# The begin of a two-block transformer kernel: x in SP's queue, 128-column sums, turned rows by k-tile

## What is computed

```python
c_act = jax.nn.silu(c)
mod = c_act @ w_ada[l] + b_ada[l]
sh_m, sc_m, gt_m, sh_f, sc_f, gt_f = jnp.split(mod, 6, axis=-1)
h = modulate(rms_norm(x, g_mix[l]), sh_m, sc_m)
proj = jnp.einsum('bsd,de->bse', h, w_in[l])
qa, ka, va, qb, kb, vb, gate_logits = jnp.split(proj, splits, axis=-1)
```

## Time and profile before

| what | us |
|---|---|
| median of three runs | 1457.21 (1453.15 to 1458.4) |
| the profiled execution | 1455.16 |
| its span in the profile | 1453.3 |
| TensorE busy | 1398.8 |
| VectorE busy | 906.8 |
| ScalarE busy | 737.4 |

### The profile page before, as it was taken

One profiled execution on the slowest core, in us unless ns is written; L12 is line 12 of the kernel. 1 busy time (PEld: TensorE's weight loads), 2 busy tenths in 40 slices (PEclk: granted clock), 3 DMA queues, 4 the chain that ended last, 5 costly groups with the idle time before them and its releaser, 6 DMA issues.

```text
span 1453.3 us, 18520 instructions
## 1 busy us (share of the span) xinstructions
PE 1398.8 (96%) x7039; PEld 1160.8 (80%) x7039; DVE 906.8 (62%) x1171; ACT 737.4 (51%) x1013; POOL 84.8 (6%) x133
## 2 busy tenths in 40 slices
PE   5999998999999999999889999999999999999998
PEld 4877876899987888887768888888888877788886
DVE  5577786688876645468876645456454555764543
ACT  4457745644546443366466444455444466564342
POOL 3011100000000000022300000000000100000000
PEclk9999999999999999999999999999999999999999
DMA  9787654577653765534335756538565463566550
GB/s 354 273 312 236 207 170 149 171 242 247 234 175 124 238 191 186 178 131 145 116 106 178 253 177 200 181 106 279 176 200 177 136 217 116 174 218 195 181 174 29
DMA packets 177592, 274.31 MB, mean 189 GB/s; under 512 B 6466, under 2 KB 120898, under 8 KB 177506
## 3 DMA queue, kind: packets, MB, share of 16 engines
q1 hardware_dynamic: 170800, 250.87, 52.3%
q0 software_dynamic: 5552, 20.20, 4.5%
q10 hardware_dynamic: 1153, 2.07, 0.4%
HBM read 272.05 MB, written 1.06 MB: 188 GB/s over the span
## 4 chain that ended last, share of the span: by engine, by line
PE 49%; DVE 1%; ACT 1%; issue 0%; POOL 0%; DVEq 0%; POOLq 0%; ACTq 0%
PE psum L2466 15%; PE psum L2468 15%; PE psum L2467 15%; PE psum L2711 1%; PE psum L2635 1%; PE psum L2563 0%; PE psum L2664 0%; PE psum L2617 0%; DVE attn L2238 0%; PE psum L2616 0%; PE psum L2578 0%; POOL scr L1801 0%; ACT w_hi L1866 0%; DVE attn L2291 0%; ACT junk L1932 0%
## 5 line engine op out<-in xcount | busy, mean ns | idle before, releaser
L2065 DVE TENSOR_TENSOR w_lo<-raw,w_hi 128x2048 fp32r<-128x2048 f32 (+1 forms) x158 | 359.7, 2279 | 187.0 <-ACT w_hi L1866 186.3
L2466 PE MATMUL psum<-w_hi,hT_hi 128*128 128x512 f32 x912 | 366.7, 402 | 9.4 <-DVE hT_lo L2161 3.5
L1866 ACT ACTIVATE w_hi<-raw 128x2048 fp32r<-128x2048 f32 (+1 forms) x158 | 299.7, 1899 | 121.8 <-PE psum L2468 80.7
L2468 PE MATMUL psum<-w_hi,hT_lo 128*128 128x512 f32 x912 | 357.2, 392 | 0.0
L2467 PE MATMUL psum<-w_lo,hT_hi 128*128 128x512 f32 x912 | 357.1, 392 | 0.0
L2466 PEld LDWEIGHTS psum<-w_hi,hT_hi 128*128 128x128 f32 x912 | 172.8, 190 | 49.7 <-issue 12.6
L2468 PEld LDWEIGHTS psum<-w_hi,hT_lo 128*128 128x128 f32 x912 | 172.7, 189 | 37.1
L2467 PEld LDWEIGHTS psum<-w_lo,hT_hi 128*128 128x128 f32 x912 | 173.2, 190 | 33.7 <-issue 0.5
L2065 DVE TENSOR_TENSOR lo_qk<-raw,hi_qk 128x2048 fp32r<-128x2048 f32 (+1 forms) x35 | 79.3, 2264 | 40.2 <-ACT hi_qk L1866 40.1
L2065 DVE TENSOR_TENSOR lo_at<-raw,hi_at 128x2048 fp32r<-128x2048 f32 x35 | 80.2, 2290 | 35.4 <-ACT hi_at L1866 35.4
L2466 PE MATMUL psum<-w_hi,hc_hi 128*128 128x512 f32 x256 | 100.5, 393 | 0.8 <-DVE hc_lo L2386 0.4
(11 more groups left out here) (234 smaller groups left out, 2312.1 us busy)
## 6 DMA issues: line engine op xcount, KB each, us to landing
raw<-in_ffn_wg_dram SPq DMA_DIRECT2D x88, 512.0 KB, 3.9
raw<-in_ffn_wu_dram SPq DMA_DIRECT2D x88, 512.0 KB, 4.9
raw<-in_ffn_wd_dram SPq DMA_DIRECT2D x44, 1024.0 KB, 4.9
raw<-in_w_up_dram SPq DMA_DIRECT2D x44, 512.0 KB, 4.9
raw<-in_w_in_dram SPq DMA_DIRECT2D x19, 1024.0 KB, 7.2
ada_raw<-in_w_ada_dram POOLq DMA_DIRECT2D x24, 512.0 KB, 5.2
raw<-in_even_w_in_dram SPq DMA_DIRECT2D x12, 1024.0 KB, 5.0
raw<-in_odd_w_in_dram SPq DMA_DIRECT2D x12, 1024.0 KB, 5.1
```

The lines of the kernel that those rows point to most:

```text
L1866: nc.scalar.activation(hi_of(s), raw_of(s), ACT.Copy)\
L2065: nc.vector.tensor_tensor(lo_of(s), raw_of(s), hi_of(s).bitcast(F32), ALU.subtract).then_inc(lo_ready, 1)
L2466: nc.tensor.matmul(o, a_hi, b_hi, start=start, stop=False)
L2468: return nc.tensor.matmul(o, a_lo, b_hi, start=False, stop=stop)
```

## The change

- **Loads.** x is loaded by SP, between the first and the second part of `w_ada`, and no longer by POOL. The fourth early part comes in two loads of 512 KB with a semaphore for each half, and DVE waits for the second half ahead of its third operation.
- **Units.** `ka`'s first half and `qa`'s second half are each cut into two units of two k-tiles. Unit numbers shift: 0 and 1 are `qa`'s first half, 2 and 3 `ka`'s, 4 `va`'s, 5 and 6 `qa`'s second half, 7 `ka`'s, 8 `va`'s.
- **Column sums.** Both kinds of products have 128 equal columns instead of one, into 128 columns of the bank, and add up in place, so that DVE adds the bias in one operation instead of two.
- **Turned rows.** A group of two k-tiles gets a step for each k-tile: two pieces on ACT, one low part of 256 columns on DVE, and a count of its own for TensorE to wait on.
- **Warm products.** 24 in three places: eight after the condition vector, ten after the vectors are turned, six after the sums of round one.
- **Order.** The vectors are copied out by ACT; the statistics stand after the first part's sum. In round one the finish of sum 0 stands ahead of the last part of `w_ada`, and unit 1 is split between the two groups of turned rows. In round two all of `va`'s first half stands between the sums and turns.

```diff
+    pl.add("warm", bank=7, times=8)
+    st = tile_stat()
+    squared = x_squares(st, (0, 1), [("x_loaded", 16)] * TT)
+    pl.add("vectors", uses=vector_uses)
+    var(st, (0, 1), squared, False, EPS)
     shared = shared_ada(0, 0, 3)
-    vector_uses = [pl.use(b) for b in (4, 5, 6, 7)]
-    pl.add("vectors", uses=vector_uses)
-    st = x_stats([("x_loaded", 16)] * TT)
-    pl.add("warm", use=vector_uses[3], times=8)
+    pl.add("normalise", st=st, half=0)
+    pl.add("warm", bank=1, times=10)
+    turned_rows = [turn_early(G, ("scr_ready", scr_version()), ("mod", 1), ("mod", 0), 0, 2),
+                   turn_early(G, None, ("mod", 1), ("mod", 0), 2, 3)]
     ada(2, 0)
-    pl.add("normalise", st=st, half=0)
-    rest = turn_early(G, ("scr_ready", scr_version()), ("mod", 1), ("mod", 0), 0, (2, 3))
+    adasum(0, shared=shared)
     shared2 = shared_ada(2, 1, 3)
-    first = first_units([(0, 0, 2), (0, 2, 2), (1, 0, 4), (2, 0, 4), (0, 4, 4), (1, 4, 4), (2, 4, 4)])
+    first = first_units([(0, 0, 2), (0, 2, 2), (1, 0, 2), (1, 2, 2), (2, 0, 4), (0, 4, 2), (0, 6, 2), (1, 4, 4), (2, 4, 4)])
     pl.split_to(0)
-    adasum(0, shared=shared)
+    adasum(2, shared=shared2)
+    pl.add("warm", bank=0, times=6)
+    pl.add("modfinal", vec=1, gain=0, half=0)
+    turned_rows[0]()
     pl.split_to(1)
-    adasum(2, shared=shared2)
-    pl.add("modfinal", vec=1, gain=0, half=0)
-    rest[0]()
-    pl.split_to(2)
-    rest[1]()
+    turned_rows[1]()
+    pl.split_to(3)
...
-            pool.dma_start(X[:, :, :], x[0].rearrange("(t p) d -> p t d", p=P)).then_inc(x_loaded, 16)
...
+                    if e == 1:
+                        sp.dma_start(X[:, :, :], x[0].rearrange("(t p) d -> p t d", p=P)).then_inc(x_loaded, 16)
+                    if e % FIRST == FIRST - 1:
+                        sp.dma_start(view[:, 0:2, :], parts[0][2][:, 0:2, :]).then_inc(early_landed[e % FIRST], 16)
+                        sp.dma_start(view[:, 2:4, :], parts[0][2][:, 2:4, :]).then_inc(early_second, 16)
...
-                                nc.tensor.matmul(psum[:, use.bank, 4 + j:5 + j],
+                                nc.tensor.matmul(psum[:, use.bank, j * P:(j + 1) * P],
                                                  w[:, k * BANK + j * P:k * BANK + (j + 1) * P],
-                                                 c_act[:, 4 + k:5 + k], start=k == a["own"][0], stop=k == 3)
+                                                 c_act[:, 4 + k:5 + k].to_broadcast([P, P]),
+                                                 start=j == 0 and k == a["own"][0], stop=False, skip_group_check=True)
```

More of the change, by code:

```diff
@@ L351, in turn_group @@
         made = pl.turned_use(bank, buffered=bias is not None)
-        pl.add("turn", src=src, after=after, scale=scale, bias=bias, kt=kt, nk=nk, ts=ts, early=False, kept=None,
+        pl.add("turn", src=src, after=after, scale=scale, bias=bias, kt=kt, nk=nk, ts=ts, early=False, i0=0, kept=None,
                free=[hT_until[t] for t in ts if hT_until[t] is not None], **made)
@@ L356, in turn_group, with turn_early, go @@
                 G[k, t] = made["g"]
-    def turn_early(G, after, scale, bias, kt, banks):
-        later = []
-        for j, bank in enumerate(banks):
-            made = pl.turned_use(bank, buffered=True)
-            kw = dict(src="scr", after=after if j == 0 else None, scale=scale, bias=bias, kt=kt + 2 * j, nk=2, ts=(0, 1),
-                      kept=None, free=[], **made)
-            pl.add("turnrows", **kw)
-            later.append(kw)
-            for k in range(kt + 2 * j, kt + 2 * j + 2):
-                for t in range(TT):
-                    G[k, t] = made["g"]
-        return [lambda kw=kw: pl.add("turn", early=True, **kw) for kw in later]
+    def turn_early(G, after, scale, bias, kt, bank):
+        made = pl.turned_use(bank, buffered=True)
+        kw = dict(src="scr", after=after, scale=scale, bias=bias, ts=(0, 1), free=[], kept=None, **made)
+        pl.add("turnrows", kt=kt, nk=2, **kw)
+        pl.turned += 1
+        second = dict(kw, ti=pl.turned - 1, g=pl.turn(), buf_free=None)
+        made["use"].read_by = ("turned_ready", pl.turned)
+        pl.buffered[-1] = second["g"]
+        for t in range(TT):
+            G[kt, t], G[kt + 1, t] = made["g"], second["g"]
+        def go():
+            pl.add("turn", early=True, kt=kt, nk=1, i0=0, **kw)
+            pl.add("turn", early=True, kt=kt + 1, nk=1, i0=1, **second)
+        return go
     def turn(src, after, scale, bias, k0=0, nk=KT, banks=(4, 5, 6, 7), G=None):
@@ L1548, in program @@
         ada_landed = [sem(f"ada_landed{i}") for i in range(2)]
-        early_landed = [sem(f"early_landed{i}") for i in range(FIRST)]
+        early_landed, early_second = [sem(f"early_landed{i}") for i in range(FIRST)], sem("early_second")
         c_act_ready = sem("c_act_ready")
@@ L1610, in wait_past, with wait_second_rows @@
                     wait_ready(eng, f)
+        def wait_second_rows(eng, what):
+            e = plan.early.index(what[1]) if what not in raw_slot else 0
+            if e % FIRST == FIRST - 1:
+                eng.wait_ge(early_second, 16 * (e // FIRST + 1))
         def wait_rows(eng, what):
@@ L2103, in _ @@
                             dve.wait_ge(ada_landed[k // 2], 16 * (a["own"] + 1))
+                        if a["own"] is None and k == 2:
+                            wait_second_rows(dve, what)
                         w = rows_in[:, k * BANK:(k + 1) * BANK]
@@ L2548, in _ @@
                         for j in range(4):
-                            ins = nc.tensor.matmul(psum[:, use.bank, j:j + 1], acc[:, j * P:(j + 1) * P],
-                                                   ones[:, 0:1], start=True, stop=True)
+                            ins = nc.tensor.matmul(psum[:, use.bank, j * P:(j + 1) * P], acc[:, j * P:(j + 1) * P],
+                                                   ones[:, 0:P], start=a["unit"] is None and j == 0, stop=True,
+                                                   skip_group_check=True)
                     ins.then_inc(psum_ready[use.bank], 1)
```

71 lines of the change are left out of this document (40 added, 31 removed).

## The result

| what | before | after |
|---|---|---|
| median of 20 runs each, side by side | 1455.73 (1453.15 to 1458.52) | 1459.36 (1456.42 to 1461.15) |
| ratio of the runs | | 1.0022, 95% interval 1.0015 to 1.0029 |
| the profiled execution, its span | 1455.16, 1453.3 | 1460.26, 1458.7 |

The changed kernel is 3.6 slower. That is within the 0.5% that the prediction called no change, but the interval leaves 1 out, the sign is the other one, and the time lies 1.9 above the range.

The account below looks back on a forecast made before the run. TensorE, busy for 96% of the span, was taken to bound the kernel. A gain of 2.75 ahead of `ka`'s second half gave 1452.4 from the profiled run, 1454.5 from the median; named 1453, range 1448.5 to 1457.5.

Parts of the forecast that it names:

- the sign: Whole kernel: faster, with a gain of 2.75 by the second half of `ka`; within 0.5% given 0.90.
- I take as that point the start of the second half of `ka`.: At 60.00 before: TensorE runs through unchanged work from there; start forecast at 57.25, gain 2.75.
- at 33.7, just when ACT is free: Landing of `va`'s load in SP's queue: unit 3 lands 3.9 after issue, then 2.7 per MB, giving 33.7.
- rival 2: SP's load queue runs dry; unit 4 lands at 36.3, its split ends 2.55 later: 1455, no change; chance 0.17.
- Round one: First round of `w_ada` sums to first product: gains 1.1, modfinal near 24.8, first product near 26.3, not 28.76.
- Rival 1: At both first column sums the clock stays low: 4.7 against a gain of 2.75, 1.95 slower, 1457.1; chance 0.13.
- Round two: Second round of `w_ada` sums on DVE: modfinal at 48.3 against 47.74, 0.55 later; two waits and a split in line.
- The gap ahead of the second half of `ka`: On TensorE after `qa`'s second half: a new wait of 1.4, shown as 1 to 2, started by unit 7's split.
- Free edits: Later wide sums cost 0 (bounds 0 and 3.4); added loads come ahead of need; warm products lie under waits.

Follow-up runs that it names:

- with the fetches back: Changed kernel with the fifth and sixth part of `w_ada` ahead of unit 3 in SP's loads and 189 waits on TensorE: 1455.49, ratio 1.0001 to before.
- the fifth and sixth part ahead: Changed kernel with the fifth and sixth part of `w_ada` ahead of unit 3 in SP's list of loads: 1457.85, ratio 1.0012 to before.
- 189 waits: Changed kernel with 189 more wait instructions on TensorE, so 256 instructions ahead of before: 1455.72, ratio 0.9998 to before.
- 67 waits: Kernel before with 67 more wait instructions on TensorE, no work added, while it waits for the vectors: 1458.61, ratio 1.0015 to before.
- 13 warm products: Changed kernel with 13 more identity products on TensorE ahead of `va`'s first k-tile, in the gap of 3.32: 1458.12, ratio 1.0017 to before.
- 156 waits: Changed kernel with 156 more wait instructions on TensorE and eight warm products ahead of the sum of `n` = 4: 1456.16, ratio 1.0004 to before.

## Why the prediction was wrong, point by point

- **"I take as that point the start of the second half of `ka`."** From that point TensorE was to run through unchanged work, so that the end moves by what the begin saves. This step failed, and with it the next one; in the profiles they weigh the same. At that point the changed kernel is 4.0 behind the forecast (61.27 against 57.25), which is the load of unit 4 and the gap below; from there to the end it loses another 4.0 against before (1.27 becomes 5.3). Two things speak against it. The work is the same, but the instructions lie 67 further on, and the fetches with them: 2.2 to 2.8 of loss with no work added. And the stretch from 60 to 90 is not TensorE's: with the fetches back and a lead of 1.35 at 60, the bias' landing and the sum of `n` = 4 took all of it. The wait of 0.75 at 87.41 stood in the trace, and the prediction has no term for it, though it was a sign that a load decides there.
- **Unit 4 "at 33.7, just when ACT is free".** 35.50. I had the dry queue in rival 2 and took it as no delay. The fifth part, unit 3 and POOL's `g_row` all had to pass behind it. Rival 2's mechanism came, at its landing of 36.3 less 0.8, but it was priced at 1455, since it had only the split in it.
- **The gap's price.** The prediction names none between `ka` and `va`; by its own numbers it would be 0.7 (48 products of 0.227 from 26.3 end at 37.2, unit 4 is split at 37.9). It was 3.32, and no term stood for the clock behind a gap: 1.7 at the second half of `ka`, 0.7 to 1.2 of the time.
- **Round one.** Right, and on the careful side: statistics 13.49 (13.7), the finish of sum 0 at 19.43 with a wait of 0.66 (20.6 with 1.5), modfinal 23.40 (24.8), first product 25.28 (26.3) at the high level.
- **Rival 1, the clock through the sums.** Did not come: the eight row turns at 16.44 took 1.10 and the sums behind them ran at 1.00. The Trainium skill, TensorE: Matmul & The Clock Gate, Part 4, says that transposes don't count as activity; here, behind ten warm products, the granted clock stayed at 1.00 through the turns (16 to 20), so in this case the rule does not decide.
- **Round two.** With unit 4 late, DVE waited 3.00 for sum 1 and modfinal came at 51.95 (48.3). With the fifth and sixth part ahead the wait was 1.43 and the second half of `ka` started at 58.01 (57.25): the working was sound once the load was there.
- **The gap ahead of the second half of `ka`**, 1 to 2: there, 1.35, with the releaser that was named.
- **"Free edits".** 24 warm products were costed by the time they take. Sixteen of them are new, and each leaves two records of products and two of weight loads: 64 of the 67 instructions that move the fetches. For that no term stood.
- **The sign.** "Wrong if the half of `ka` starts after 60, or if DMA is the releaser of unit 4's high part by more than 1": both happened, so the text's own tests show the begin wrong. Nothing in it looked behind 60. That the change stays within 0.5% was right, but not for its reasons: no gain came.

What stays open: how the 3.6 divides between fetches and the begin, since 189 waits changed both. By parts it is 2.2 to 2.8 from the place of the instructions (67 waits) and 0.7 to 1.2 from the gap's clock (13 warm products); that the two add up in the changed kernel is assumed. That 156 waits took 3.4 off with a gap and the low clock still there speaks for the fetches as the larger part. How much of it arises at 87, where the half of `ada_raw` came late in some kernels without a fetch too, is open as well. Why half-clock windows near 710 in before are missing in the changed kernel was not tried.

## What to carry to other kernels

In a kernel without loops on the busy engine, every instruction added moves all later instruction fetches; before crediting or blaming an edit at the begin, compare where the fetches fall against the loads that are waited for, or run the old kernel with as many idle waits, and fill up to a whole block to get the old places back. A lead gained early is worth only what the next load-bound wait lets through, so look for that wait, however small, before taking the gain to the end. Where a reorder lets the load queue run dry, the bytes that then stand in line set the landing, not the time of issue.

## What the runs showed of the hardware

- With one fetch of 16 KB (0.9 to 1.7 by the trace's packets) beside it, the second load of the `w_up` pair landed 0.9 to 1.6 later, in all ten kernels in which one fell there (5.86 to 6.58 after issue, 4.95 in before), and in none of the eight others (4.88 to 5.22).
- The delay was that of one part of sixteen: in those ten the last part came 0.9 to 1.4 behind the fifteenth, in before and the eight others 0.2 at most.
- At the half of `ada_raw` it is less plain: 5.66 to 7.45 after issue in the eleven kernels with a fetch beside it, 4.69 to 6.20 in the eight without.
- The place of the fetches repeats to 0.1 between two kernels that differ by 256 instructions on TensorE (11.1 and 7.51 against 11.04 and 7.58).
- At 287, 1.2 more of waiting (1.33 before, 2.53 with 67 waits) went with a granted clock of 0.50 instead of 1.00 in the window behind.
